# Attention scores of a two-block kernel on one core: every pair of heads' scores over all 128 rows of the array, with the residual h parked in DRAM to make room

## The chip, the core and the metric

The kernel runs on one core of one Trainium2 chip. Its program is written engine by engine: TensorE (PE) multiplies, VectorE (DVE) and ScalarE (ACT) work on the results, SyncE (SP) and GpSimd (POOL) issue the transfers, and semaphores tie them together. The metric is the device time of the core in microseconds, as the median of several executions; lower is better.

## What is computed

Two blocks run one after the other on 512 tokens of width 1024. The change lies in the first block, in its attention. Cut to that part:

```python
h = x
h = h + 0.5 * swiglu(rms_norm(h, ffn1_norm), ffn1_w1, ffn1_w3, ffn1_w2)
proj = rms_norm(h, mix_norm) @ w_in            # q, k, v of 12 heads of 64, pool input, gates
q, k = apply_partial_rope(q), apply_partial_rope(k)
for g, (window, dilation) in enumerate(((128, 1), (512, 4), (2048, 16))):   # 4 heads each
    s = q_g @ k_g.T * 64 ** -0.5               # banded and causal, key stride = dilation
    o_g, lse_g = softmax(s) @ v_g, log-sum-exp of s
o = sum_g softmax_g(lse_g) * o_g
h = h + (gate0 * (o @ w_branch_attn) + gate1 * (pool(proj) @ w_branch_pool)) @ w_out
h = h + 0.5 * swiglu(rms_norm(h, ffn2_norm), ffn2_w1, ffn2_w3, ffn2_w2)
```

All is float32 outside, and each product is made from two parts of each operand: a high part in a rounded float32 format (fp32r), and a low part that holds the rest. A product of split operands is three matmuls: high by high, high by low, low by high.

## The kernel before

**Stages.** The first feed-forward layer ends with h complete (tile h, 128 partitions x 8 x 512, 2 MB). Then comes the mixing stage. Its q and k columns are projected for three head groups g, once for the first pair of heads (a = 0, `qk(False)`) and once for the second pair (a = 1, `qk(True)`). Between them stand pool rows, values, and the attention of pair 0 (`attend(0)`); after the second come values and `attend(1)`. Then the gates and branches follow, in products of seven parts (`seven`), and a loop that adds the result into h.

**q and k.** For each g and each o (0 is q, 1 is k) PE projects 128 columns, both heads of the pair below each other, 64 rows each. ACT and DVE split the result (`rope_split`, `rope_low`) for two rotation matmuls (`rotate`), DVE multiplies by the cosine, and `rope_done` finishes the step: DVE multiplies and adds, ACT makes the high part, DVE the low part. In group 0 the high part is written by two ACT instructions of 64 rows into q_both[j] and k_both[j], one tile for each head j, and the low part by two DVE instructions into q_low and k_low. In groups 1 and 2 one ACT and one DVE instruction over 128 rows do it, into qk_hi and qk_lo. `prep` splits the next weight slab (ACT w_hi, DVE w_lo), and PE may not start on a slab before that. All of this is written out by hand, and each engine runs its own list strictly in order.

**Copies on POOL.** `other_halves(a)` fills the other 64 rows of q_both[j] with the low part of q, and those of k_both[j] with k's high part once more, so that one matmul over 128 rows gives (high + low of q) by (high of k). Four transfers of 128 KB from SBUF to SBUF do it, after group 0 of each pair.

**Scores.** `scores(a, k)` serves one unit, one head and one residue of the tokens by 4; there are 8 units for each pair, 16 in all. It makes 2 mask matmuls in bf16 (L2641, L2642), then for group 0 one over 128 rows (L2643) and one over 64 rows with k_low (L2644), and for groups 1 and 2 three each over 64 rows (L2419 to L2421, reached through `passes`): 10 matmuls. Units 0 and 1 stand between value matmuls, units 2 to 7 inside `attend`, which goes round once per unit: scores of unit k + 3, transposes of unit k + 1 (L2658), probabilities by values of unit k (L2683). ACT's list of a round is a quarter of a weight slab in the first four rounds (`prep_part`), two copies (`stage`), `normalizer` and `exps`; DVE has as much beside it.

**Queues.** SP issues the weight slabs in order, each when its place in the ring of two is free. POOL issues the adding transfers of the seven-part products (L571), the copies above, and copies into mix_b. Nothing reads or writes h between the end of the first feed-forward layer (with the scaling into x_hi and x_lo) and the loop that adds the mixing stage's result.

## Time and profile before

| | us |
|---|---|
| median of 3 runs | 1864.92 (1864.58 to 1866.64) |
| profiled execution | 1866.13, of which the span of its instructions 1864.1 |
| PE busy | 1850.0 (99%) |
| DVE busy | 1324.1 (71%) |
| ACT busy | 890.8 (48%) |
| POOL busy | 61.7 (3%) |
| DMA | 212.55 MB, mean 114 GB/s |
| granted TensorE clock | 0.998 |

Every row of the trace gives a start in microseconds from the beginning of the span, a duration, the engine, the line, the operation and its tiles; in square brackets stands how long the engine was idle before it and what ended that. Matmuls overlap one another, so the time that one takes on PE is read from the distance of the starts, not from its duration; the same holds for short DVE and ACT instructions, which overlap by about 0.1 us unless something holds them. The chain of waits is the chain of work that ended last: it goes through whichever engine was late at each moment.

### The profile page before, as it was taken

The numbers are of one execution on the slowest core, as the hardware profiler recorded it, in microseconds if no ns is written. First come the engines' busy times: TensorE is split into PE (matmuls) and PEld (weight loads), VectorE is DVE, ScalarE is ACT, GpSimd is POOL, SyncE is SP. The second block draws the span as 40 slices with busy tenths as digits, with TensorE's granted clock in tenths as the row PEclk, the third lists the DMA queues.
The fourth block names the chain that finished last, engine by engine and source line by source line (L and its number), as shares of the span: only waits on it lengthen the run. The fifth ranks groups of instructions, "written<-read, shape, count | busy, mean of one in ns | idle before, by whom it ended". The sixth has DMA issues, their size and how long they took to land.

```text
span 1864.1 us, 27146 instructions
## 1 busy us (share of the span) xinstructions
PE 1850.0 (99%) x10799; PEld 1627.6 (87%) x10799; DVE 1324.1 (71%) x1786; ACT 890.8 (48%) x1182; POOL 61.7 (3%) x80
## 2 busy tenths in 40 slices
PE   9999999999999999999999999999999999999997
PEld 7998998888889988989998888888888888888886
DVE  8875887887678889856888745463646776666666
ACT  6652664436365536634653342433336644444445
POOL 0000000010000000000000000000000000000000
PEclk9999999999999999999999999999999999999999
DMA  6744763341216426654753222122221222212213
GB/s 214 184 124 125 196 171 101 132 125 69 74 55 176 141 98 163 169 161 123 193 151 112 102 81 101 68 90 72 105 84 56 91 84 75 90 69 89 90 68 91
DMA packets 49633, 212.55 MB, mean 114 GB/s; under 512 B 5648, under 2 KB 8240, under 8 KB 38144
## 3 DMA queue, kind: packets, MB, share of 16 engines
q1 hardware_dynamic: 38816, 178.80, 28.1%
q0 software_dynamic: 10288, 31.84, 9.0%
q8 instruction: 68, 1.11, 0.2%
q10 hardware_dynamic: 432, 0.56, 0.1%
q14 instruction: 29, 0.24, 0.0%
HBM read 203.32 MB, written 3.67 MB: 111 GB/s over the span
## 4 chain that ended last, share of the span: by engine, by line
PE 94%; DVE 3%; ACT 1%; issue 1%; DMA 0%; DVEq 0%; ACTq 0%
PE acc L2419 20%; PE acc L2420 20%; PE acc L2421 20%; PE acc L2425 7%; PE acc L2426 7%; PE acc L2427 7%; PE att L2420 2%; PE att L2421 2%; PE att L2419 2%; PE att L2425 1%; PE att L2427 1%; PE att L2426 1%; PE acc L2683 1%; PE acc L2658 1%; DVE w_lo L1350 0%
## 5 line engine op out<-in xcount | busy, mean ns | idle before, releaser
L1350 DVE TENSOR_TENSOR w_lo<-raw,w_hi 128x2048 fp32r<-128x2048 f32 (+1 forms) x120 | 271.4, 2262 | 69.8 <-ACT w_hi L642 68.9
L642 ACT ACTIVATE w_hi<-raw 128x2048 fp32r<-128x2048 f32 (+1 forms) x120 | 226.5, 1888 | 120.4 <-PE acc L2421 105.6
L2419 PE MATMUL acc<-x_hi,w_hi 128*128 128x512 f32 x712 | 280.3, 394 | 0.3 <-DVE tmp L1578 0.3
L2421 PE MATMUL acc<-x_hi,w_lo 128*128 128x512 f32 x712 | 277.4, 390 | 0.0
L2420 PE MATMUL acc<-x_lo,w_hi 128*128 128x512 f32 x712 | 277.3, 389 | 0.0
L2419 PEld LDWEIGHTS acc<-x_hi,w_hi 128*128 128x128 f32 x712 | 133.7, 188 | 30.9 <-issue 2.7
L2420 PEld LDWEIGHTS acc<-x_lo,w_hi 128*128 128x128 f32 x712 | 133.7, 188 | 28.4 <-issue 1.2
L2421 PEld LDWEIGHTS acc<-x_hi,w_lo 128*128 128x128 f32 x712 | 133.6, 188 | 28.0
L2425 PE MATMUL acc<-xt_hi,w_hi 128*128 128x256 f32 x516 | 144.6, 280 | 0.0
L2427 PE MATMUL acc<-xt_hi,w_lo 128*128 128x256 f32 x516 | 144.3, 280 | 0.0
L2426 PE MATMUL acc<-xt_lo,w_hi 128*128 128x256 f32 x516 | 144.3, 280 | 0.0
L2420 PE MATMUL acc<-g_lo,w_hi 128*128 128x512 f32 x352 | 137.0, 389 | 0.0
L2419 PE MATMUL acc<-g_hi,w_hi 128*128 128x512 f32 x352 | 137.0, 389 | 0.0
L2421 PE MATMUL acc<-g_hi,w_lo 128*128 128x512 f32 x352 | 136.9, 389 | 0.0
L741 ACT ACTIVATE tmp<-acc 128x256 f32<-128x256 f32 x172 | 65.4, 380 | 78.9 <-PE acc L2427 71.4
L2425 PEld LDWEIGHTS acc<-xt_hi,w_hi 128*128 128x128 f32 x516 | 98.1, 190 | 0.0
L2426 PEld LDWEIGHTS acc<-xt_lo,w_hi 128*128 128x128 f32 x516 | 96.9, 188 | 0.0
L2427 PEld LDWEIGHTS acc<-xt_hi,w_lo 128*128 128x128 f32 x516 | 96.9, 188 | 0.0
L2425 PE MATMUL acc<-x_hi,wc_hi 128*128 128x256 f32 x344 | 95.1, 276 | 0.0
L2427 PE MATMUL acc<-x_hi,wc_lo 128*128 128x256 f32 x344 | 95.0, 276 | 0.0
L2426 PE MATMUL acc<-x_lo,wc_hi 128*128 128x256 f32 x344 | 95.0, 276 | 0.0
L2419 PEld LDWEIGHTS acc<-g_hi,w_hi 128*128 128x128 f32 x352 | 66.1, 188 | 13.7
(477 smaller groups left out, 4665.4 us busy)
## 6 DMA issues: line engine op xcount, KB each, us to landing
raw<-in_ret_head SPq DMA_DIRECT2D x24, 1024.0 KB, 4.8
raw<-in_ffn_down SPq DMA_DIRECT2D x32, 704.0 KB, 4.1
raw_c<-in_ffn_seven SPq DMA_DIRECT2D x37, 512.0 KB, 5.3
raw<-in_ffn_seven SPq DMA_DIRECT2D x33, 512.0 KB, 4.7
raw<-in_ffn_seven POOLq DMA_DIRECT2D x33, 512.0 KB, 7.5
raw<-in_ffn_seven SPq DMA_DIRECT2D x37, 256.0 KB, 4.5
raw<-in_ret_out SPq DMA_DIRECT2D x8, 1024.0 KB, 4.7
raw<-in_sb_v SPq DMA_DIRECT2D x8, 1024.0 KB, 4.7
```

The costliest lines, as they stand in the source:

```text
L642: nc.scalar.activation(w_hi[:, slot, at:at + cols], raw[:, slot, 0:cols], ACT.Copy).then_inc(w_hi_ready, 1)
L741: nc.scalar.activation(dst, src, ACT.Copy).then_inc(snap_ready, 1)
L1350: tt(w_lo[:, slot, at:at + cols], raw[:, slot, 0:cols], w_hi[:, slot, at:at + cols].bitcast(F32), ALU.subtract).then_inc(w_ready, 1)
L2419: mm(dst, still[0], move[0], start=first, stop=False)
L2420: mm(dst, still[0], move[1], start=False, stop=False)
L2421: return mm(dst, still[1], move[0], start=False, stop=last)
L2425: mm(dst, still[0], move[0], start=first, stop=False, skip_group_check=True)
L2426: mm(dst, still[0], move[1], start=False, stop=False, skip_group_check=True)
L2427: return mm(dst, still[1], move[0], start=False, stop=last, skip_group_check=True)
L2658: last = nc.tensor.transpose(dst[i // TB][:, P * (i % TB):P * (i % TB) + P], tmp[:, at:at + P], ident[:])
L2683: last = mm(dst, va[:, k_blk, value_slot(g, head)].rearrange("p s d -> p (s d)"), turned_probs[:, k % 2, i].rearrange("p s q -> p (s q)"), ...
```

## The change

All three groups are treated as group 0 was, and k's low part gets a second half of zeros, so that every scores product is two matmuls over 128 rows: (q high, q low) by (k high, k high), and (q high, q low) by (k low, zeros). That is 8 matmuls a unit in place of 10. q_both and k_both grow to three groups each. k_rest (the low part of k with zeros) and two of the three q_low tiles lie where h lies. So h is written to DRAM once it is complete (h_parked, 2 MB, by SP) and read back by POOL in four transfers of 512 KB between the adding transfers of the first four seven-part products. POOL also clears two halves of k_rest.

```diff
+        with ExitStack() as under:
+            k_rest = [sb(f"k_rest{j}", [P, N_GROUPS, TOK], F32R, under) for j in range(2)]
+            q_low = [sb(f"q_low{g}", [P, TOK], F32R, under) for g in range(N_GROUPS - 1)]
         h = sb("h", [P, DC, TOK])
+        h_parked = nc.dram_tensor("h_parked", (P, DC, TOK), F32, kind="Internal").ap()
...
         with ExitStack() as under:
-            k_low = sb("k_low", [P, TOK], F32R, under)
+            q_low.append(sb("q_low_last", [P, TOK], F32R, under))
...
             for g in range(N_GROUPS):
                 fetch(dram["mix_qk"][0, g])
+            sp.wait_ge(h_ready, DC)
+            sp.dma_start(h_parked, h[:]).then_inc(park_landed, 16)
...
+            pool.wait_ge(park_landed, 16)
+            pool.wait_ge(seg_done, FFN_SEGS[0] + 1)
+            for j, rows in enumerate(head_rows[::-1]):
+                nc.gpsimd.memset(k_rest[j][rows, :, :].bitcast(F32), 0.0).then_inc(rest_clear, 1)
...
                 own, other = head_rows, head_rows[::-1]
-                pool.wait_ge(both_ready, 2 * a + 1)
-                for j in range(2):
-                    pool.dma_start(q_both[j][other[j], :], q_low[own[j], :]).then_inc(both_landed, 16)
-                pool.wait_ge(both_ready, 2 * a + 2)
-                for j in range(2):
-                    pool.dma_start(k_both[j][other[j], :], k_both[j][own[j], :]).then_inc(both_landed, 16)
+                for g in range(N_GROUPS):
+                    done = 2 * (N_GROUPS * a + g)
+                    pool.wait_ge(both_ready, done + 1)
+                    for j in range(2):
+                        pool.dma_start(q_both[j][other[j], g, :], q_low[g][own[j], :]).then_inc(both_landed, 16)
+                    pool.wait_ge(both_ready, done + 2)
+                    for j in range(2):
+                        pool.dma_start(k_both[j][other[j], g, :], k_both[j][own[j], g, :]).then_inc(both_landed, 16)
...
                     add_pair(dram["mix_seven"][2 * j + k - MIX_PLAIN], slab)
                     v.next()
+                    if j < 3:
+                        pool.wait_ge(prob_ready, 2 * UNITS)
+                        rows = slice(2 * (2 * (j - 1) + k), 2 * (2 * (j - 1) + k) + 2)
+                        pool.dma_start(h[:, rows, :], h_parked[:, rows, :]).then_inc(h_back, 16)
...
-                if g:
-                    ins = nc.scalar.activation(qk_hi[:, o, g - 1, :], t(o), ACT.Copy, scale=QK_SCALE[o])
-                else:
-                    for j, rows in enumerate(head_rows):
-                        ins = nc.scalar.activation((k_both if o else q_both)[j][rows, :], t(o)[rows, :], ACT.Copy, scale=QK_SCALE[o])
+                for j, rows in enumerate(head_rows):
+                    ins = nc.scalar.activation((k_both if o else q_both)[j][rows, g, :], t(o)[rows, :], ACT.Copy, scale=QK_SCALE[o])
...
-                if g:
-                    stt(qk_lo[:, o, g - 1, :], t(o), QK_SCALE[o], qk_hi[:, o, g - 1, :].bitcast(F32), ALU.mult, ALU.subtract).then_inc(op_ready, 1)
-                else:
-                    for j, rows in enumerate(head_rows):
-                        stt((k_low if o else q_low)[rows, :], t(o)[rows, :], QK_SCALE[o], (k_both if o else q_both)[j][rows, :].bitcast(F32),
-                            ALU.mult, ALU.subtract).then_inc(both_ready if j else op_ready, 1)
-                    dve.wait_ge(both_ready, both.next())
+                if both.k == 0:
+                    dve.wait_ge(park_landed, 16)
+                for j, rows in enumerate(head_rows):
+                    dst, high = (k_rest[j][rows, g, :], k_both[j][rows, g, :]) if o else (q_low[g][rows, :], q_both[j][rows, g, :])
+                    stt(dst, t(o)[rows, :], QK_SCALE[o], high.bitcast(F32),
+                        ALU.mult, ALU.subtract).then_inc(both_ready if j else op_ready, 1)
+                dve.wait_ge(both_ready, both.next())
...
             rope_done(N_GROUPS - 1, 1, 0)
-            dve.wait_ge(both_landed, 4 * 16)
...
             sq.next()
+            dve.wait_ge(h_back, 4 * 16)
...
-                mm(wide, both[:, plain[r]], keys[:], start=False, stop=False)
-                mm(wide, both[rows, plain[r]], k_low[rows, :], start=False, stop=True)
-                for g in range(N_GROUPS - 1):
-                    last = passes(narrow[:, P * g:P * (g + 1)], (q[0][:, g, :], q[1][:, g, :]),
-                                  (qk_hi[rows, 1, g, plain[r]], qk_lo[rows, 1, g, plain[r]]), False, g == N_GROUPS - 2)
+                q, high, rest = q_both[head], k_both[head], k_rest[head]
+                mm(wide, q[:, 0, plain[r]], high[:, 0, :], start=False, stop=False)
+                mm(wide, q[:, 0, plain[r]], rest[:, 0, :], start=False, stop=True)
+                for g in range(1, N_GROUPS):
+                    dst = narrow[:, P * (g - 1):P * g]
+                    mm(dst, q[:, g, plain[r]], high[:, g, plain[r]], start=False, stop=False)
+                    last = mm(dst, q[:, g, plain[r]], rest[:, g, plain[r]], start=False, stop=g == N_GROUPS - 1)
...
                 pe.wait_ge(op_ready, op.at())
-                pe.wait_ge(both_landed, 4 * 16 * (a + 1))
+                pe.wait_ge(rest_clear, 2)
+                pe.wait_ge(both_landed, 4 * N_GROUPS * 16 * (a + 1))
                 scores(a, 0)
```

What it does to DVE's list at group 1 of q (a = 0), from the w_lo of the slab before to the next step; tmp holds the rotated q, L1374 is the low part of the next projection. Before:

```order
L1350 TENSOR_TENSOR w_lo<-raw,w_hi 128x2048 [waits w_hi_ready]
L1698 TENSOR_TENSOR tmp<-att,rope_a 128x512 [waits att_full]
L1701 TENSOR_TENSOR tmp<-tmp 128x512 [waits acc_free,att_free]
L1704 SCALAR_TENSOR_TENSOR qk_lo<-tmp,qk_hi 128x512 [waits hi_ready]
L1374 TENSOR_TENSOR stage<-acc,stage 128x512 [waits hi_ready,op_ready]
```

and after:

```order
L1362 TENSOR_TENSOR w_lo<-raw,w_hi 128x2048 [waits w_hi_ready]
L1710 TENSOR_TENSOR tmp<-att,rope_a 128x512 [waits att_full]
L1713 TENSOR_TENSOR tmp<-tmp 128x512 [waits acc_free,att_free]
L1719 SCALAR_TENSOR_TENSOR q_low<-tmp,q_both 64x512 [waits hi_ready]
L1719 SCALAR_TENSOR_TENSOR q_low<-tmp,q_both 64x512
L1386 TENSOR_TENSOR stage<-acc,stage 128x512 [waits hi_ready,op_ready,both_ready]
```

One instruction has become two of half the rows, and the next one waits for the second of them too; it is so at q and k of groups 1 and 2, four times for each pair.

PE's list at the first unit of a pair (`first_score`), masks first. Before:

```order
L2641 MATMUL att<-band,ident_b 128x512 [waits att_free,both_landed,op_ready]
L2642 MATMUL att<-classes,ident_b 128x256
L2643 MATMUL att<-k_both,q_both 128x512
L2644 MATMUL att<-k_low,q_both 128x512
L2419 MATMUL att<-qk_hi 128x128
L2420 MATMUL att<-qk_lo,qk_hi 128x128
L2421 MATMUL att<-qk_hi,qk_lo 128x128
L2419 MATMUL att<-qk_hi 128x128
L2420 MATMUL att<-qk_lo,qk_hi 128x128
L2421 MATMUL att<-qk_hi,qk_lo 128x128
```

and after:

```order
L2651 MATMUL att<-band,ident_b 128x512 [waits both_landed,att_free,rest_clear,op_ready]
L2652 MATMUL att<-classes,ident_b 128x256
L2654 MATMUL att<-k_both,q_both 128x512
L2655 MATMUL att<-k_rest,q_both 128x512
L2658 MATMUL att<-k_both,q_both 128x128
L2659 MATMUL att<-k_rest,q_both 128x128
L2658 MATMUL att<-k_both,q_both 128x128
L2659 MATMUL att<-k_rest,q_both 128x128
```

The two groups' three products have become two each, and the unit now waits for the copies of all three groups (the sizes are those of the outputs; the rows of the array don't show in them).

## Rows read from the trace of the kernel before

**Rows 1.** The page, busy time, share and instructions of each engine.

```profile
PE 1850.0 (99%) x10799; PEld 1627.6 (87%) x10799; DVE 1324.1 (71%) x1786; ACT 890.8 (48%) x1182; POOL 61.7 (3%) x80
```

**Rows 2.** Timeline of PE: one round of attend(0), then the transposes; start, duration.

```profile
445.57 0.39 PE L2641 MATMUL att<-band,ident_b 128*128 128x512 bf16 x1
445.80 0.27 PE L2642 MATMUL att<-classes,ident_b 128*128 128x256 bf16 x1
...
446.23 0.50 PE L2644 MATMUL att<-k_low,q_both 64*128 64x512 f32 x1
446.57 0.22 PE L2419 MATMUL att<-qk_hi 64*128 64x128 f32 x1
...
447.08 0.27 PE L2421 MATMUL att<-qk_hi,qk_lo 64*128 64x128 f32 x1
447.28 0.88 PE L2658 MATMUL acc<-ident,tmp 128*128 128x128 f32 x6
```

**Rows 3.** Timeline of DVE from the first rope_done to the value slab.

```profile
373.94 1.41 DVE L1707 SCALAR_TENSOR_TENSOR k_low<-tmp,k_both 64x512 fp32r<-64x512 f32 x2 [1.34 <-ACT k_both L875]
375.38 0.69 DVE L1374 TENSOR_TENSOR stage<-acc,stage 128x512 fp32r<-128x512 f32 x1
...
380.89 0.69 DVE L1704 SCALAR_TENSOR_TENSOR qk_lo<-tmp,qk_hi 128x512 fp32r<-128x512 f32 x1 [0.70 <-ACT qk_hi L872]
381.62 0.69 DVE L1374 TENSOR_TENSOR stage<-acc,stage 128x512 fp32r<-128x512 f32 x1
...
390.77 2.29 DVE L1350 TENSOR_TENSOR w_lo<-raw,w_hi 128x2048 fp32r<-128x2048 f32 x1 [1.11 <-ACT w_hi L642]
...
405.02 2.28 DVE L1350 TENSOR_TENSOR w_lo<-raw,w_hi 128x2048 fp32r<-128x2048 f32 x1
```

**Rows 4.** Timeline of PE: the first matmul on the value slab.

```profile
407.36 0.39 PE L2419 MATMUL acc<-w_hi,x_hi 128*128 128x256 f32 x1
```

**Rows 5.** Timeline of ACT: before the second pool slab, and between scores and values.

```profile
388.30 0.63 ACT L872 ACTIVATE qk_hi<-tmp 128x512 fp32r<-128x512 f32 x1 [2.92 <-DVE tmp L1701]
...
428.09 0.84 ACT L901 ACTIVATE va<-acc,r_tok 128x256 fp32r<-128x256 f32 x2 [0.81 <-PE acc L2421]
```

**Rows 6.** Timeline of ACT in attend(0): first and fourth quarter slab, then two stages.

```profile
441.47 0.62 ACT L652 ACTIVATE w_hi<-raw 128x512 fp32r<-128x512 f32 x1
...
450.43 0.64 ACT L652 ACTIVATE w_hi<-raw 128x512 fp32r<-128x512 f32 x1
...
454.25 0.60 ACT L931 ACTIVATE stage<-acc 128x512 fp32r<-128x512 f32 x1 [0.56 <-PE acc L2658]
...
457.11 0.60 ACT L931 ACTIVATE stage<-acc 128x512 fp32r<-128x512 f32 x1 [0.28 <-PE acc L2658]
```

**Rows 7.** Chain of waits through qk(True): start, duration, engine, tile, line.

```profile
471.66 0.47 issue
...
502.49 0.70 DVE qk_lo L1704
503.24 0.39 PE att L2641
```

**Rows 8.** Timeline of POOL, and the transfers of tile k_both: the copies.

```profile
375.64 1.03 POOL L596 DMA_DIRECT2D k_both<-k_both  x2 [4.21 <-DVE k_low L1707]
...
DMA to landing us min/median/max: 2.2/2.3/2.5
```

**Rows 9.** The last update of h; landing of 512 KB copies (mix_b); a POOL clear.

```profile
348.65 0.69 DVE L1633 TENSOR_TENSOR h<-h,tmp 128x512 f32<-128x512 f32 x1
...
DMA to landing us min/median/max: 3.4/6.8/13.7
...
1030.88 3.53 POOL L618 MEMSET y_ret<- 128x4096 f32 x1 [57.31 <-PE acc L2421]
```

**Rows 10.** Timelines of DVE and ACT at the second seven-part product.

```profile
581.42 1.22 DVE L1457 TENSOR_TENSOR w_lo<-raw,w_hi 128x1024 fp32r<-128x1024 f32 x1
...
586.10 0.36 ACT L741 ACTIVATE tmp<-acc 128x256 f32<-128x256 f32 x1
```

More of the change, by code:

```diff
@@ L127, in block_kernel @@
         x_lo = sb("x_lo", [P, DC, TOK], F32R)
-        with ExitStack() as under:
-            sb("tmp_first", [P, 4 * TOK], F32, under)
-            q_low = sb("q_low", [P, TOK], F32R, under)
         tmp = sb("tmp", [P, 6 * TOK])
         with ExitStack() as under:
-            k_low = sb("k_low", [P, TOK], F32R, under)
+            q_low.append(sb("q_low_last", [P, TOK], F32R, under))
         ssq = sb("ssq", [P, TOK])
@@ L252, in block_kernel @@
             with ExitStack() as inner:
-                q_both = [sb(f"q_both{j}", [P, TOK], F32R, inner) for j in range(2)]
-                k_both = [sb(f"k_both{j}", [P, TOK], F32R, inner) for j in range(2)]
-                qk_hi = sb("qk_hi", [P, 2, N_GROUPS - 1, TOK], F32R, inner)
-                qk_lo = sb("qk_lo", [P, 2, N_GROUPS - 1, TOK], F32R, inner)
+                q_both = [sb(f"q_both{j}", [P, N_GROUPS, TOK], F32R, inner) for j in range(2)]
+                k_both = [sb(f"k_both{j}", [P, N_GROUPS, TOK], F32R, inner) for j in range(2)]
                 va = sb("va", [P, TB, N_GROUPS * GROUP_HEADS, 2, HEAD], F32R, inner)
@@ L408, in block_kernel @@
         both_landed = sem("both_landed")
+        park_landed = sem("park_landed")
+        rest_clear = sem("rest_clear")
+        h_back = sem("h_back")
         mix_copied = sem("mix_copied")
@@ L2631, in scores @@
             def scores(a, k):
-                r, rows = k // 2, slice(HEAD * (k % 2), HEAD * (k % 2) + HEAD)
+                r, head = divmod(k, 2)
                 if k >= 2:
@@ L2638, in scores @@
                 b.next(2)
-                q = qk_hi[rows, 0, :, plain[r]], qk_lo[rows, 0, :, plain[r]]
-                both, keys = q_both[k % 2], k_both[k % 2]
                 mm(wide, ident_b[:], by_rows(band[:, DIL - 1 - r:2 * DIL - 1 - r, :]), start=True, stop=False)
                 mm(narrow[:, 0:2 * P], ident_b[:], by_rows(classes[:]), start=True, stop=False)
-                mm(wide, both[:, plain[r]], keys[:], start=False, stop=False)
-                mm(wide, both[rows, plain[r]], k_low[rows, :], start=False, stop=True)
-                for g in range(N_GROUPS - 1):
-                    last = passes(narrow[:, P * g:P * (g + 1)], (q[0][:, g, :], q[1][:, g, :]),
-                                  (qk_hi[rows, 1, g, plain[r]], qk_lo[rows, 1, g, plain[r]]), False, g == N_GROUPS - 2)
+                q, high, rest = q_both[head], k_both[head], k_rest[head]
[5 more added lines that the diff above has]
+                    last = mm(dst, q[:, g, plain[r]], rest[:, g, plain[r]], start=False, stop=g == N_GROUPS - 1)
                 last.then_inc(att_full, 2)
```

## The prediction

> **What bounds the kernel now.** I read the busy shares first, then the chain of waits over the mixing stage, then the timelines of PE, DVE and ACT at the places where the chain leaves PE. PE is busy 99% of the span and DVE 71% [rows 1], so nearly everywhere PE's own list sets the time. The average hides three places inside the mixing stage. In qk(False) PE doesn't visibly wait, but DVE has no slack to give: it runs its list through with no pause but its waits for ACT, its w_lo of the value slab ends at 405.02 + 2.28 = 407.30, and PE's first matmul on that slab starts at 407.36 [rows 3, 4]. In qk(True) the chain itself lies on DVE and ACT, from the end of the first projection at 471.66 to the last low part, 502.49 + 0.70 = 503.19; the first unit of pair 1 starts at 503.24 [rows 7]. In the first four rounds of attend ACT is full: from its first quarter slab at 441.47 to its fourth at 450.43 are three rounds of 2.99 us without a pause [rows 6].
>
> **What a unit of scores costs, and will cost.** Before, 1.71 us: 445.57 to 447.28 [rows 2]. Of this 0.23 and 0.43 are the two masks and the first group-0 product, which stay. The rest is 1.05 us: 0.34 for the 64-row product L2644, 0.51 from the first to the sixth narrow one (0.10 each), 0.20 from the sixth to the transposes. After: a 128-row product of 512 columns, for which I take the 0.23 of the mask of the same width, and four narrow ones at 0.11, together 0.67. Saving 0.38, call it 0.4. The bounds are 0.2 (only two narrow matmuls fewer, and the long steps round the 64-row products stay) and 0.55 (the 0.43 before them shrinks as well, and so does the first step of what follows). I stay near the middle, because the two long steps, 0.34 and 0.20, are just those where 64-row and 128-row matmuls meet, and after the change none meet. Sixteen units give 6.4 us if PE were the bound at all of them; it isn't.
>
> The Trainium skill, "TensorE: Matmul & The Clock Gate", section "Back-to-back issue gap", gives about 81 ns for a sustained matmul of 128 columns; the trace has 0.10 [rows 2], and by the page's figure a unit would save 0.1 us more, at the units that count about 0.3 us in all.
>
> **What the split into 64-row halves costs.** The pair at k of group 0 takes DVE from 373.94 to 375.38, 1.44 us, the single one of group 1 from 380.89 to 381.62, 0.73: 0.71 more. DVE waits 1.34 us for ACT's pair and 0.70 for the single copy: 0.64 more [rows 3]. So each `rope_done` of groups 1 and 2 costs DVE 1.35 us. There are four for each pair, eight in all.
>
> The Trainium skill, "VectorE: DVE Perf Modes", section "Two Vector instructions with no wait between them", says that an instruction whose output starts in another quarter of the partitions than the last is held until the earlier ones are done. The measured pair bears this out (1.44, two full durations of 0.69 and more). Without it two halves would follow one another as overlapping instructions do and the step would cost about 0.1 us less each; it speaks against the change.
>
> *Pair 0.* Three of the four steps cost 1.35. At the last but one, ACT makes w_hi of the second pool slab next, and DVE waits for that: 1.11 us of pause before 390.77 [rows 3]. ACT's own delay of 0.64 passes on (its copy at 388.30 becomes two [rows 5]), but DVE's 0.71 falls into the pause. Sum 3 x 1.35 + 0.65 = 4.7. The slack at 407.36 is 0.06, so PE stands still about 4.7 us, part of it already at the second pool slab. Then PE wins 0.8 on units 0 and 1, but the next link is ACT: its va at 428.09 had waited 0.81 for PE [rows 5], and ACT itself comes 4.7 later. 4.7 - 0.8 = **+3.9** either way.
>
> *attend(0).* Up to 441 the chain runs over ACT and DVE, and for three rounds more ACT is full, so faster scores give nothing there except what ACT's first pauses behind it show: 0.56 and 0.28 [rows 6]. **-0.85**; bounds 0 and 4 x 0.4 = 1.6 (PE bound in all four rounds that still have a scores call).
>
> *Pair 1.* Here DVE's chain is the path, and the four steps lie on it: **+5.4**. The rotation of group 2's q and of its k each start later, and PE pauses there instead of later. The last low part ends at 503.19 + 5.4 = 508.6. Before, PE started 0.05 behind it. Now k's last copies stand between: POOL starts 0.29 after the pair's end (373.94 + 1.41 to 375.64), two issues of 0.52, the second lands 2.3 after its start [rows 8]: 0.29 + 0.52 + 2.3 - 0.05 = **+3.05**. Queued behind PE's wait are unit 0, the third value block and all of attend(1), while DVE uses the time for its mix_b sums. Bounds 2.0 (if landing were counted with the first issue) and 5 (the copies of 512 KB on the same queue took 3.4 to 13.7 [rows 9], though nothing else of POOL's is under way here). Then units 0 and 1 of pair 1, on PE's path: **-0.8**. attend(1) as attend(0): **-0.85**.
>
> **h.** h is complete at 349.3 [rows 9], SP has nothing to wait for, and DVE's first low pair needs the place of h only at about 368.5, the step before 373.94 [rows 3]: 19 us for 2 MB. Four copies of 512 KB at the quickest 3.4 us make 13.6, and the new transfer has no other beside it at first. Nothing lost; at the median of 6.8 us each it would be 27, and DVE 8 us late. POOL's clear covers 1536 columns twice: from 3.53 us for 4096 [rows 9], 1.3 us each, while POOL waits for q anyway; lower bound 0, upper bound 2.6 before its first copy, which has 40 us until it is used. The way back adds 2 MB between the adding transfers. The second product's w_lo is ready at 582.6, and PE begins that product at about 584.7 (its first part, 12 matmuls of 256 columns or 1.4 us, is copied at 586.10) [rows 10]: 2 us of cover against transfers of the same size as those which it crosses. I take 0, upper bound 2. It also displaces the wait for both_landed on DVE, which the trace doesn't show as a pause: 0. Behind the mixing stage nothing changes, and PE is the bound, so what has been lost is kept.
>
> **Sum.** 3.9 - 0.85 + 5.4 + 3.05 - 0.8 - 0.85 = +9.85 us. The profiled execution took 1866.13, which is 1.2 above the median; its sum is 1876.0, and against the median 1864.92 + 9.85 = **1874.8**.
>
> **Rivals.**
> *Halves on the path, less the relief (1871.5).* As above, but the scores save 0.55 a unit and attend passes on nearly all of it: 1.6 + 0.6 for each attend in place of 0.85, and 0.6 more at units 0 and 1 of pair 1. For it: the long steps round 64 rows. Against it: ACT's three full rounds.
> *Transfers late (1879).* The forecast plus 2 to 6 us: copies of the last group that land at 4 us, a parking that ends behind 368.5, or the way back showing at a seven-part product. For it: the spread of 3.4 to 13.7 us. Against it: the small copies spread by 0.3 us only.
> *Not slower (1858.5).* DVE idles 29% of the span and POOL 97%. If the halves and copies ran in that idle time, only the 16 x 0.4 us would be left. It would take more than 4.7 us between w_lo and its use at 407, and more than 8 at 503. The rows show 0.06 and 0.05, so this decides against it; it is left only if DVE's list has play that a single trace hides, as where it waits for ACT.
>
> **How the numbers follow.** Forecast 0.62 (1872.5 to 1877.5), less cost 0.12 (0.02 of it below 1868.7), transfers late 0.17, not slower 0.09 (0.05 of it faster than 1861.2, 0.04 between that and 1868.7). 0.2% or 3.7 us is about what a measurement of this kernel can tell from no change. The range from 1870.5 to 1880.5 takes in the first three but for their tails. Slower 0.89, same 0.06, faster 0.05.
>
> **What would show it.** PE standing about 4.7 us before the value slab, w_lo being what ends it; the chain through qk(True) longer by 5.4; PE waiting some 3 us more for a copy into k_both before the first unit of pair 1; a unit of scores at 1.3 us; rounds of attend at 3.0. If the first unit of pair 1 starts less than 6 us later than by the shift that it inherits, or the rounds fall to 2.75, I am too high. If DVE waits for the parking, too low.

## The result, and the profile after

| | before | after |
|---|---|---|
| median, us | 1865.29 (1864.58 to 1866.64, 4 runs) | 1881.61 (1881.01 to 1882.52, 4 runs) |
| ratio, with its 95% interval | | 1.0087 (1.0070 to 1.0105) |
| span of the profiled execution | 1864.1 | 1879.4 |
| granted TensorE clock, mean | 0.998 | 0.993 |
| DMA, MB | 212.55 | 218.85 |

The change makes the kernel 16.3 us slower. The sign was forecast, the size was not: I had said +9.85, and 1881.6 lies above the range. The page after has nearly the same shares; POOL has 22 instructions more, and PE fewer busy microseconds in a longer span.

The page of after, busy time of each engine, for [rows 1]:

```profile
PE 1848.6 (98%) x10761; PEld 1629.8 (87%) x10767; DVE 1330.8 (71%) x1794; ACT 895.4 (48%) x1190; POOL 74.9 (4%) x102
```

The waits of PE in after (engine, tile, line, what ended them, us in total, times, longest). Of before the same view has 0.8 us in two pieces for the first of these, and neither of the other two:

```profile
PE att L2596 <- DVE stage L1386: 5.1, 3, 3.3
PE acc L2431 <- DVE w_lo L1362: 4.4, 1, 4.4
PE att L2652 <- DMA k_both<-k_both: 4.0, 1, 4.0
```

These are the standstills that the prediction names, at the places it names. The 4.0 reach to the second mask of the first unit, because the record of its first mask is missing; PE stood some 3.6 of them. ACT's copy of o_hi, which closes each pair of heads, shows where the time is lost. It starts at 466.14 and 541.84 before. After:

```profile
471.27 0.60 ACT L937 ACTIVATE o_hi<-att 128x512 fp32r<-128x512 f32 x1 [1.12 <-PE att L2639]
...
557.20 0.60 ACT L937 ACTIVATE o_hi<-att 128x512 fp32r<-128x512 f32 x1 [3.49 <-PE att L2639]
```

That is +5.13 for pair 0 and +15.36 for both, and the spans differ by 15.3. So all of it arises up to the end of attend(1), and nothing comes or goes behind it.

Now the timeline of PE in after at the value slab of pair 0, for [rows 4]; the first line is the last matmul on the slab before, and from 412.12 on each has 256 columns:

```profile
407.37 0.39 PE L2433 MATMUL acc<-x_hi,w_lo 128*128 128x512 f32 x1
412.12 0.58 PE L2431 MATMUL acc<-w_hi,x_hi 128*128 128x256 f32 x1 [4.37 <-DVE w_lo L1362]
...
412.93 0.41 PE L2431 MATMUL acc<-w_hi,x_hi 128*128 128x256 f32 x1
413.14 0.41 PE L2432 MATMUL acc<-w_lo,x_hi 128*128 128x256 f32 x1
...
425.23 0.28 PE L2432 MATMUL acc<-w_lo,x_hi 128*128 128x256 f32 x1
425.35 0.28 PE L2433 MATMUL acc<-w_hi,x_lo 128*128 128x256 f32 x1
```

The first starts 4.76 later than before (407.36), w_lo being what ends the wait: the 4.7 of the forecast. But behind it the matmuls start 0.21 apart, and only later 0.11. The view by stretches of after says why (stretch, its length, busy time of PE, PEld, DVE, ACT and POOL with counts, PEclk, DMA share, GB/s):

```profile
408.00:412.00 4.00, 0.00 (x0) 0.00 (x0) 3.86 (x7) 2.10 (x2) 3.09 (x3) 0.79 0.35 54
412.00:414.00 2.00, 1.88 (x9) 1.88 (x10) 1.89 (x4) 0.83 (x1) 0.80 (x1) 0.50 1.19 171
414.00:416.00 2.00, 2.00 (x11) 2.00 (x11) 1.90 (x4) 0.00 (x0) 0.00 (x0) 0.50 1.14 149
416.00:418.00 2.00, 2.00 (x15) 2.00 (x15) 1.61 (x4) 0.25 (x1) 0.00 (x0) 0.71 1.15 238
418.00:420.00 2.00, 2.00 (x20) 2.00 (x19) 1.08 (x1) 0.86 (x1) 0.00 (x0) 1.00 1.25 201
```

While PE stood still its granted clock fell to 0.50, that is 1.2 in place of 2.4 GHz, and it stayed there for some 5 us of work: 9 to 11 matmuls in 2 us where the last line counts 20 at 1.00. In before the clock is 1.00 in every stretch from 406 to 420. The Trainium skill, "TensorE: Matmul & The Clock Gate", section "What's actually happening", describes just this: a gate in front of the array that halves its clock when PE has had nothing to do, and opens again under work. The trace agrees, and my prediction did not use it. The same view of after in pair 1:

```profile
510.00:512.00 2.00, 2.00 (x12) 2.00 (x11) 1.23 (x2) 0.69 (x2) 0.00 (x0) 0.50 0.40 79
...
516.00:518.00 2.00, 0.01 (x1) 0.14 (x3) 2.00 (x4) 0.00 (x0) 0.00 (x0) 0.53 0.35 72
518.00:520.00 2.00, 2.00 (x8) 1.80 (x8) 0.44 (x2) 0.00 (x0) 0.00 (x0) 0.50 0.00 0
520.00:522.00 2.00, 2.00 (x11) 2.00 (x11) 0.96 (x1) 0.89 (x2) 0.00 (x0) 0.50 0.00 0
522.00:524.00 2.00, 2.00 (x16) 2.00 (x14) 0.00 (x0) 0.10 (x2) 0.00 (x0) 0.76 0.03 8
```

The clock falls twice more: behind 3.29 us of waiting for DVE (up to 508.9), where DVE's chain is the path and a slow PE does little harm, and behind the wait for k's copies, where the first unit of scores and a value block run at half the rate with nothing to hide them.

A unit of scores in after, in the timeline of PE, for [rows 2]; the record of its first mask is missing, and the block before it ends with a matmul that starts at 425.35:

```profile
425.69 0.27 PE L2652 MATMUL att<-classes,ident_b 128*128 128x256 bf16 x1
425.72 0.48 PE L2654 MATMUL att<-k_both,q_both 128*128 128x512 f32 x1
426.04 0.39 PE L2655 MATMUL att<-k_rest,q_both 128*128 128x512 f32 x1
426.27 0.22 PE L2658 MATMUL att<-k_both,q_both 128*128 128x128 f32 x1
...
426.55 0.27 PE L2659 MATMUL att<-k_rest,q_both 128*128 128x128 f32 x1
426.66 0.33 PE L2431 MATMUL acc<-w_hi,x_hi 128*128 128x256 f32 x1
```

From 425.46 (0.11 behind that matmul) to 426.66 are 1.20 us, against 1.71 before. The Trainium skill, "TensorEngine Tiling (Array Packing)", section "Key Properties", states that a change of the tiling mode drains the array. The rows agree: the step of 0.34 at the 64-row product is 0.23 now, and the 0.20 behind the last narrow one is 0.11. No run changes the mode alone, with the number of matmuls kept.

The account of the mixing stage, forecast against trace:

| step | forecast | trace | how read |
|---|---|---|---|
| PE stands before the value slab | +4.7 | +4.76 | 407.36 to 412.12 |
| low clock behind it | none | +1.93 | to unit 0: 13.34 after, 11.41 before |
| units 0 and 1, pair 0 | -0.8 | -1.12 | va at 433.66 instead of 428.09 is +5.57 in all |
| attend(0) | -0.85 | -0.44 | +5.57 to +5.13 |
| qk(True), DVE's chain | +5.4 | +5.69 | last low part ends at 514.01, before 503.19 |
| k's last copies | +3.05 | +3.54 | first unit at about 517.6, 3.6 behind it |
| units 0 and 1, attend(1) | -1.65 | -1.56 | taken as in pair 0 |
| low clock behind the copies | none | +2.56 | what is left: 15.36 less the rows above, see below |
| sum | +9.85 | +15.36 | |

The last two rows are not read each by itself. A direct reading supports them: from the first unit of pair 1 to the second are 6.55 us in after (517.57 to 524.12) and 4.05 in e6_early_copy (517.25 to 521.30), the same work at a clock of 1.00, so the low clock cost 2.5 there. The +1.93 is a difference from before; e3_warm, with the clock at 1.00, does the same four value blocks in 11.0 us and not 11.4, and against that the low clock cost 2.3. Why its matmuls stand 0.113 us apart and those of before 0.118, both at 1.00, no run shows.

Of the 5.5 us between forecast and trace, 4.5 are the two rows that the forecast lacks.

### The profile page after: what moved, and what is told of

Its sections match the earlier page's. It is cut to its first block, busy times and chain, and to the rows that moved or that the text cites. A ratio compares the mean times of both kernels' runs of the same rounds, so it can differ in the third digit from the quotient of the medians.

```text
span 1879.4 us, 27122 instructions
## 1 busy us (share of the span) xinstructions
PE 1848.6 (98%) x10761; PEld 1629.8 (87%) x10767; DVE 1330.8 (71%) x1794; ACT 895.4 (48%) x1190; POOL 74.9 (4%) x102
## 2 busy tenths in 40 slices
DMA packets 51633, 218.85 MB, mean 116 GB/s; under 512 B 5984, under 2 KB 8576, under 8 KB 40016
## 4 chain that ended last, share of the span: by engine, by line
PE 72%; DVE 6%; ACT 2%; issue 1%; DMA 0%; DVEq 0%; POOL 0%
PE acc L2431 16%; PE acc L2433 16%; PE acc L2432 16%; PE acc L2438 4%; PE acc L2437 4%; PE acc L2439 4%; PE att L2432 2%; PE att L2433 2%; PE att L2431 2%; DVE w_lo L1362 1%; PE att L2437 1%; PE att L2439 1%; PE att L2438 1%; DVE neg_max L1753 1%; DVE tmp L1713 0%
## 5 line engine op out<-in xcount | busy, mean ns | idle before, releaser
L2431 PE MATMUL acc<-w_hi,x_hi 128*128 128x512 f32 (+1 forms) x224 | 79.6, 355 | 4.4 <-DVE w_lo L1362 4.4
```

The lines of the kernel that those rows point to most:

```text
L2431: mm(dst, still[0], move[0], start=first, stop=False)
```

## Experiments

Each kernel ran beside the kernel before on the same chip. Differences are of medians; the interval is that of the ratio to before. The last column compares medians that were not taken side by side: the kernel before itself lay between 1865.1 and 1865.9 in these rounds, so differences there are good to somewhat under 1 us. The edits are shown in part.

| kernel | median, us | ratio to before | against before | against after |
|---|---|---|---|---|
| e1_park | 1866.56 | 1.0003 (0.9993 to 1.0012) | +0.7 | |
| e2_halves | 1877.84 | 1.0064 (1.0047 to 1.0080) | +12.0 | -3.8 |
| e3_warm | 1877.75 | 1.0063 (1.0046 to 1.0080) | +11.9 | -3.9 |
| e5_relief | 1863.18 | 0.9984 (0.9974 to 0.9993) | -2.7 | |
| e4_stagger | 1873.89 | 1.0043 (1.0026 to 1.0060) | +8.4 | -7.7 |
| e6_early_copy | 1877.66 | 1.0063 (1.0046 to 1.0080) | +12.1 | -4.0 |
| e7_all_three | 1871.41 | 1.0029 (1.0016 to 1.0042) | +5.9 | -10.2 |
| e8_before_step | 1864.79 | 0.9995 (0.9986 to 1.0005) | -0.7 | |
| e9_pool_half | 1875.15 | 1.0049 (1.0032 to 1.0066) | +9.3 | -6.5 |
| e10_stagger_early | 1872.54 | 1.0034 (1.0021 to 1.0046) | +6.7 | -9.1 |
| e11_stagger_early_warm | 1871.53 | 1.0033 (1.0021 to 1.0044) | +5.7 | -10.1 |
| e12_no_standing | 1869.94 | 1.0027 (1.0015 to 1.0038) | +4.8 | -11.7 |

### The parts, each by itself on the kernel before

The parking alone:

```
+            sp.wait_ge(h_ready, DC)
+            sp.dma_start(h_parked, h[:]).then_inc(park_landed, 16)
...
+                    if j < 3:
+                        pool.wait_ge(prob_ready, 2 * UNITS)
+                        rows = slice(2 * (2 * (j - 1) + k), 2 * (2 * (j - 1) + k) + 2)
+                        pool.dma_start(h[:, rows, :], h_parked[:, rows, :]).then_inc(h_back, 16)
```

> The kernel before with only the parking of h: the 2 MB copy to DRAM behind the third mix_qk slab on SP, the four copies back between POOL's adding transfers, DVE's two waits for them. Nothing of the scores changes. My theory (the transfers are hidden, all of the loss is made of DVE's halves, the wait for k's copies and TensorE's lower clock behind both): within 0.5 us of before. Rival (the 4 MB more of traffic cost something in slabs that land later, or in the way back): 2 to 6 us slower, with a new DMA or h_back wait on DVE or PE. The changed kernel itself shows no such wait, so I expect the first.

Measured +0.7 with an interval of -1.3 to +2.2 us, and in the profile no wait of PE or DVE for a transfer of h. The 4 MB cost nothing that can be told.

The split alone (ACT likewise):

```
-                    stt(qk_lo[:, o, g - 1, :], t(o), ...).then_inc(op_ready, 1)
+                    for j, rows in enumerate(head_rows):
+                        stt(qk_lo[rows, o, g - 1, :], t(o)[rows, :], ...).then_inc(both_ready if j else op_ready, 1)
```

> The kernel before with only the split: groups 1 and 2 get their high part (ACT) and low part (DVE) in two halves of 64 rows each, with DVE's wait for the second; scores, copies and h as before. Theory: PE stands still about 4.8 us before the first value slab, the granted clock is 0.50 behind it and the four value blocks take 1.9 us more; in pair 1 the chain through DVE is 5.5 us longer, and there is no wait for copies. Sum 4.8 + 1.9 + 5.5 = +12.2 us, about 1877. Rival A (the clock has nothing to do with the standstill, but with the copies or the 128-row scores): granted clock 1.00 behind it, +10.3, about 1875. Rival B (halves hide in idle time): within 1 us of before.

Measured +12.0, where the theory had +12.2. The interval, +8.8 to +14.9, rules out rival B but would hold rival A's +10.3; what speaks against A is the granted clock, which falls behind the wait although the scores still run over 64 rows and no copy is added. The timeline of PE and the stretches around it in e2_halves:

```profile
412.37 0.58 PE L2422 MATMUL acc<-w_hi,x_hi 128*128 128x256 f32 x1 [4.34 <-DVE w_lo L1351]
```

```profile
412.00:414.00 2.00, 1.63 (x7) 1.63 (x8) 1.89 (x4) 1.08 (x1) 0.00 (x0) 0.50 0.28 71
414.00:416.00 2.00, 2.00 (x14) 2.00 (x13) 1.93 (x3) 0.00 (x0) 0.00 (x0) 0.67 0.17 65
416.00:418.00 2.00, 2.00 (x20) 2.00 (x19) 1.81 (x5) 0.02 (x1) 0.00 (x0) 1.00 0.00 0
```

Here it lasts some 3 us, in the profile of after 5: the price of the same wait varies. The pieces of this profile are 5.0 of standing, 1.1 of low clock (ACT's o_hi of pair 0 starts 6.16 later than before) and 5.5 in pair 1 (o_hi there 11.66 later).

The relief on PE alone:

```
...
-                mm(wide, both[rows, plain[r]], k_low[rows, :], start=False, stop=True)
+                mm(wide, both[:, plain[r]], k_low[:, :], start=False, stop=True)
...
-                    last = passes(narrow[:, P * g:P * (g + 1)], (q[0][:, g, :], q[1][:, g, :]),
-                                  (qk_hi[rows, 1, g, plain[r]], qk_lo[rows, 1, g, plain[r]]), False, g == N_GROUPS - 2)
+                    dst = narrow[:, P * g:P * (g + 1)]
+                    mm(dst, qk_hi[:, 0, g, plain[r]], qk_hi[:, 1, g, plain[r]], start=False, stop=False)
+                    last = mm(dst, qk_hi[:, 0, g, plain[r]], qk_lo[:, 1, g, plain[r]], start=False, stop=g == N_GROUPS - 2)
```

> The kernel before with only the relief on PE: a unit of scores issues the changed kernel's matmuls (two of 512 columns and four of 128, all over 128 rows) on the tiles that the kernel before has. This leaves out part of the computation: groups 1 and 2 sum over both heads of a pair and lack one low product, and group 0's low product takes rows of both heads. Nothing else changes. Theory: a unit takes 1.2 to 1.3 us in place of 1.71; units 0 and 1 of pair 0 give 0.8 (then ACT is the bound), attend(0) 0.45, units 0 and 1 of pair 1 give 1.1, attend(1) 0.45: -2.8 us, about 1862.5. My forecast's terms sum to -3.3. Rival (PE is the bound at all sixteen units): 16 x 0.45 = -7.2, about 1858.

Measured -2.7, the theory's -2.8. So this is what the change has to give: 0.45 to 0.5 us a unit, of which 16 units let a third through. The three parts add up to +10.0. The change is +16.3; the 6.3 between are put down to the copies, 3.5 of waiting and 2.6 of low clock by the account above. That is a difference of runs, with the spread of each in it; no run adds the copies alone.

### The clock, by itself

PE is given matmuls whose result nobody reads while it would stand still:

```
+            def keep_busy(n):
+                pe.wait_ge(att_free, b.at(1))
+                for i in range(n):
+                    mm(att[:, b.k % BANKS, :], rot_r[:], x_hi[:, i % DC, :], start=True, stop=True)
...
+                if behind:
+                    keep_busy(14)
                 pe.wait_ge(op_ready, op.at(behind))
...
+            keep_busy(17)
             values(x, plain)
...
+                if a:
+                    keep_busy(26)
                 pe.wait_ge(op_ready, op.at())
```

> The changed kernel, with matmuls whose result nobody reads put where PE stands still: 17 of 512 columns before the first value slab of pair 0, 14 before the last rotation of pair 1, 26 before its first scores. No one's work moves otherwise. Theory (the granted clock fell to 0.50 because PE stood still, and this costs 1.9 us behind the value slab and 2.6 us behind the wait for k's copies): clock near 1.00 at both places and 4 to 5 us faster than the changed kernel, about 1877. Rival (the lower clock there has another cause, or costs nothing since others set the time): 1881 to 1882, or slower where the added matmuls run past the end of the wait.

Measured -3.9 against after, and the executions don't overlap (1877.6 to 1878.6 against 1881.0 to 1882.5). The timeline of PE in e3_warm, and its stretches there and in pair 1:

```profile
408.24 4.12 PE L2632 MATMUL att<-x_hi,rot_r 128*128 128x512 f32 x17
412.71 0.39 PE L2431 MATMUL acc<-w_hi,x_hi 128*128 128x256 f32 x1 [0.34 <-DVE w_lo L1362]
```

```profile
412.00:414.00 2.00, 1.66 (x13) 1.29 (x12) 1.89 (x4) 1.43 (x1) 1.41 (x2) 1.00 1.21 182
...
518.00:520.00 2.00, 2.00 (x19) 2.00 (x19) 0.96 (x1) 0.50 (x1) 0.00 (x0) 1.00 0.00 0
```

The value slab still comes when DVE has made it, at 412.7, but what follows runs at 1.00 at once. This settles that the clock falls because PE stands still, and that the low clock costs about 4 us on top of the standstills. It is a lower bound: the 26 matmuls before the first scores of pair 1 run on until 517.0, while the second copy is issued at 513.81 and in after PE starts 2.4 behind that issue, so some 0.8 us of them are too many. The 57 added matmuls, whose result nobody reads, make the kernel faster.

### Where the halves cost: ACT and DVE one behind the other

```
-                    ins = nc.scalar.activation((k_both if o else q_both)[j][rows, g, :], ...)
-                ins.then_inc(hi_ready, 1)
+                    nc.scalar.activation((k_both if o else q_both)[j][rows, g, :], ...).then_inc(half_ready[j], 1)
...
-                dve.wait_ge(hi_ready, hi.next())
...
                 for j, rows in enumerate(head_rows):
+                    dve.wait_ge(half_ready[j], both.k + 1)
```

> The changed kernel, but DVE no longer waits for both of ACT's halves before its own: each half of ACT raises a semaphore of its own, and DVE starts the first low half while ACT makes the second high half. The halves stay as many and as long. Theory (the 1.35 us a step of my forecast is made of 0.64 of waiting and 0.71 of DVE work, and the path runs through both): each of the twelve steps gives 0.6 to 0.65 back, in pair 0 at least five of six, so PE stands still about 1.5 us in place of 4.8 and the clock stays at 1.00 behind it, 3.2 + 1.9; in pair 1 six steps, 3.7; the wait for k's copies and the low clock behind it stay. Sum -8.8 us against the changed kernel, about 1872.8. Rival (it is DVE's work alone that counts, waiting hides): under 1 us.

Measured -7.7 against after where -8.8 was expected. The timeline of DVE in e4_stagger, beside [rows 3]: the pair is as long as before, the wait ahead of it is 0.70 in place of 1.34.

```profile
373.12 1.41 DVE L1719 SCALAR_TENSOR_TENSOR k_rest<-tmp,k_both 64x512 fp32r<-64x512 f32 x2 [0.70 <-ACT k_both L888]
```

And PE's wait at the value slab is half as long (timeline of PE):

```profile
410.03 0.39 PE L2431 MATMUL acc<-w_hi,x_hi 128*128 128x256 f32 x1 [2.21 <-DVE w_lo L1362]
```

The miss of 1.1 is the clock again: I had expected none to be lost behind this shorter wait. It fell, and the four value blocks behind it take 12.6 us (410.03 to 422.66) against 11.4 in before:

```profile
410.00:412.00 2.00, 1.97 (x11) 1.97 (x12) 1.89 (x3) 0.73 (x1) 1.60 (x2) 0.61 1.22 186
412.00:414.00 2.00, 2.00 (x11) 2.00 (x11) 1.90 (x4) 0.00 (x0) 0.00 (x0) 0.53 1.17 158
```

### k's copies

```
-                    pool.wait_ge(both_ready, done + 2)
                     for j in range(2):
+                        pool.wait_ge(half_ready[j], done + 2)
...
+                pe.wait_ge(both_ready, 2 * N_GROUPS * (a + 1))
                 pe.wait_ge(both_landed, 4 * N_GROUPS * 16 * (a + 1))
```

> The changed kernel, but k's copies on POOL wait for ACT's high halves, which they copy, and no longer for DVE's low halves behind them; PE waits for those itself. Theory (the copies' latency lies on the path before the first unit of pair 1): both copies start earlier by DVE's two halves of 0.72, so PE's wait for k_both shrinks from 4.0 to 2.6 us: -1.4 us, about 1880; and if the shorter standstill keeps the clock at 1.00 behind it, another -2.6, about 1877.5. Rival (something else holds PE there): no change.

Measured -4.0, which is the larger of the two cases, but by other pieces. In the profile the second copy is issued 2.1 us sooner against DVE's last low part than in after, since the first no longer waits for ACT's second half either, and PE stands 1.4 us in place of some 3.6 (waits of PE; here the first mask is on record); behind that the clock is 1.00 (stretches):

```profile
PE att L2652 <- DMA k_both<-k_both: 1.4, 1, 1.4
```

```profile
516.00:518.00 2.00, 0.75 (x4) 0.61 (x5) 1.97 (x2) 0.74 (x2) 0.00 (x0) 1.00 0.28 56
```

The 2.1 and the 2.6 of the clock would be 4.7. In this profile PE reached the value slab of pair 0 0.9 later than in after, which I can't explain, and the clock stayed low for longer behind it (some 6 us), so that o_hi of pair 0 comes 1.4 later; pair 1 by itself is 4.2 shorter than in after.

### Together, and what they uncover

The move of the first two units:

```
-            values(x, plain, {(0, DC - 1): lambda: rotate_last(1), (1, DC - 1): lambda: first_score(1),
-                              (2, DC - 1): lambda: scores(1, 1)})
+            values(x, plain, {(0, DC - 1): lambda: rotate_last(1), (2, DC - 1): lambda: first_score(1),
+                              (3, DC - 1): lambda: scores(1, 1)})
```

> The changed kernel with the staggered halves, k's early copies, and in pair 1 the first two units of scores one value block later (behind the third and fourth block in place of the second and third), so that a block of 2.7 us lies under the copies' latency. Theory: -8.8 of the stagger, -1.4 of the early copy, -2.6 of the block under what remains of the wait, and -2.6 since the clock no longer falls: 1881.6 - 15.4 = 1866, level with the kernel before. Rival (the losses overlap, so that taking one away uncovers the next): 1869 to 1873. A further rival: the later first unit leaves ACT too little time before the first transposes of attend(1), 1 to 2 us given back.

Measured 1871.4, not 1866: both rivals came. The timeline of PE at the start of attend(1) in e7_all_three:

```profile
517.55 0.87 PE L2670 MATMUL acc<-ident,tmp 128*128 128x128 f32 x6 [0.89 <-ACT tmp L928]
521.32 0.84 PE L2670 MATMUL acc<-ident,tmp 128*128 128x128 f32 x6 [1.53 <-DVE va L1438]
```

The wait for the copies is gone (0.3 us are left), but with the first unit one block later ACT and DVE are late for the first transposes by 2.4 us. A third wait of 0.95 follows at 523.1, and behind these three the clock falls, though none of them is longer than 1.53:

```profile
522.00:524.00 2.00, 1.05 (x6) 0.92 (x5) 1.87 (x5) 1.93 (x5) 0.00 (x0) 0.69 0.00 0
```

In the 2 us after these it is 0.50. It fell behind the 2.22 us before the value slab too (0.53 and 0.61 in the two stretches from 410). The sum of 15.4 had put down nothing for either.

> The changed kernel with the staggered halves and k's early copies, units of scores where they were. Theory (the wait for k's copies, and the clock behind it, come on top of the halves): the same 4 us less than with the stagger alone as the early copies gave on the changed kernel: 1873.9 - 4 = 1870. Then moving the first units of pair 1 one block later has brought nothing or lost 1 us (1871.4), since the wait it removed came back in front of attend(1). Rival (the move was worth its 2 us): 1873.

Measured 1872.5 with executions from 1869.8 to 1873.4, between the two cases: the median says that the move of the units was worth 1.1 us, the spread says that this isn't shown. In the profile PE stood 2.2 us before the value slab as in e4_stagger, and this time kept its clock:

```profile
410.00:412.00 2.00, 1.61 (x13) 1.61 (x14) 1.89 (x4) 1.11 (x1) 1.55 (x2) 1.00 1.23 185
412.00:414.00 2.00, 2.00 (x19) 2.00 (x18) 1.93 (x3) 0.00 (x0) 0.00 (x0) 1.00 1.16 152
```

Up to there this kernel and e7_all_three are the same. So at this length of wait the fall comes in one execution and not in another. The four executions of e9_pool_half show what may hang on it: 1873.35 and 1874.61 us at a mean clock of 0.998, 1875.69 at 0.996 and 1876.95 at 0.995. Only the last has a trace; its waits before the value slab, the last rotation and the first scores are 4.6, 2.5 and some 3.4 us.

> The same, with matmuls whose result nobody reads in the two standstills that are left: 8 of 512 columns before the value slab of pair 0 (2.2 us of waiting there), 7 before the last rotation of pair 1 (2.0 us). Theory (the clock fell to 0.50 behind the 2.2 us, and that alone costs 1.5 to 2 us there): the clock stays at 1.00 and the time falls by 1.5 to 2 us against the same kernel without them, to about 1868. Rival (at 2 us the low clock costs nothing on the path): no difference.

Measured -1.0 against e10_stagger_early, with ranges that overlap: not shown either way. This run could hardly show it: in the profile of e10_stagger_early the clock was kept at that place without added matmuls, and the wait for the copies was left open (3.4 us, clock 0.50 behind it).

> The kernel with staggered halves, early copies and added matmuls at two places, with 14 more of 512 columns before the first scores of pair 1, where PE still stood 3.4 us and the granted clock was 0.50 behind it. Theory (the spread of 3 us between executions of the kernels with staggered halves, 1870.4 to 1873.2, comes from the clock, which falls behind such a wait in some executions for longer than in others): mean clock 0.998 as before, all executions within about 1 us, median 1869.5 to 1870. If the halves and copies cost nothing but what is left of DVE's chain, this is the floor of the change as it is, 4 us above the kernel before. Rival (the spread has another cause, or the low clock is no loss there): the median stays at 1871.5 and the spread at 3 us.

Measured 1869.9, mean clock 0.998 to 0.999 in all seven executions; six lie between 1869.5 and 1870.6. The seventh, 1871.9, had the full clock too, so the clock isn't the whole of the spread. 4.8 us above before remain. The median is 1.6 below that of e11_stagger_early_warm (0.9 with each taken against its own kernel before), and the ranges overlap in part (1869.5 to 1871.9 and 1870.4 to 1873.2). In the profile ACT's o_hi starts at 467.44 and 546.08, 1.3 and 4.2 later than before: pair 0 is nearly even, and in pair 1 what is left of DVE's chain and the copies' latency outweighs the relief; how the two share it no run shows.

### Half of the work on POOL

```
+                    nc.gpsimd.tensor_tensor(q_low[g][rows, :], t(0)[rows, :], q_both[1][rows, g, :].bitcast(F32), ALU.subtract)
...
+                    nc.gpsimd.tensor_tensor(k_rest[1][rows, g, :], t(1)[rows, :], k_both[1][rows, g, :].bitcast(F32), ALU.subtract)
```

> The changed kernel with the staggered halves and k's early copies, and with the second low half of each step (of q and of k) on POOL in place of DVE; q's scale of 1/8 moves from ACT's and DVE's halves into DVE's two steps before them, an exact power of two. DVE waits for POOL's half before it writes the buffer that POOL reads. Theory (what counts is DVE's time a step: one wait of 0.7 for ACT's first half and one low half of 0.7 are 1.4, as much as before in groups 1 and 2 and half of it in group 0): no wait for w_lo before the value slab, clock 1.00 there, and pair 1's chain 3 us shorter than before, with some 2 us of wait for k's copies left. About 1861 to 1865, if POOL needs no more than about 1 us for 64x512 elements (its clear took 1.4 us for 128x1536, a simpler operation). Rival (POOL needs 2 us or more, and DVE waits for it, six times in each pair): every further us costs about 10; 1870 or more.

Measured 1875.2, inside the rival's range though POOL needs less than its 2 us, so not for its reason alone. POOL's half takes 1.3 us (groups of instructions on POOL: shapes, count, busy us, mean ns, idle before), against 0.7 on DVE, and DVE waits for it and for ACT (timeline of DVE):

```profile
L615 POOL TENSOR_TENSOR k_rest<-tmp,k_both 64x512 fp32r<-64x512 f32 x6 | 7.9, 1324 | 0.1
```

```profile
386.59 0.69 DVE L1393 TENSOR_TENSOR stage<-acc,stage 128x512 fp32r<-128x512 f32 x1 [0.66 <-ACT stage L686]
388.27 0.69 DVE L1710 TENSOR_TENSOR tmp<-acc,rope_a 128x512 f32<-128x512 f32 x1 [0.99 <-POOL k_rest L615]
```

The 0.66 is there as well: with its own second half gone, DVE comes to the next step before ACT has finished its two copies and that step's high part. ACT's pair costs time on DVE's path even with DVE's second half gone. How the rest of the time divides is not shown.

### The staggered halves on the kernel before

> The kernel before with the staggered halves alone, in its group 0, where it has them already: two steps in each pair. Theory (in pair 1 the path runs through ACT's and DVE's steps, in pair 0 PE has no wait to lose): 2 x 0.6 = -1.2 us, about 1864.5, at the limit of what can be told from no change. Rival (all four count): -2.5, about 1863.

Measured -0.7, interval 0.9986 to 1.0005, which is -2.6 to +0.9 us: it holds the theory's -1.2, the rival's -2.5 and no change alike, and decides nothing. No kernel here is measurably faster than the one before but e5_relief, which leaves out part of the computation.

## Why the prediction was too low

**What bounds the kernel, and where it waits.** Right at all three places: PE stopped where [rows 4] had 0.06 us of slack and [rows 7] had 0.05, and DVE's w_lo, DVE's chain and the copy ended the waits. The rival "not slower" is refuted by e2_halves, the rival "transfers late" by e1_park for the parking and the way back, and by the trace of after for k's last copy, which landed in 2.2 us: its time, 1879, is near, but its mechanism isn't there. The rival "less the relief" had the size of a unit right (0.55, measured 0.51), but attend passed on less and not more.

**The split.** Right: +4.76 for 4.7, +5.69 for 5.4. The chain of waits shows the step at q of group 1 in qk(True), first before (start, duration, engine, tile, line), 1.4 us from ACT's copy to the end of DVE's low part:

```profile
490.71 0.64 ACT qk_hi L872
...
491.37 0.70 DVE qk_lo L1704
```

and then after, two copies of ACT and two low parts of DVE in a row, the 2.7 us that the steps of group 0 had in [rows 3]:

```profile
495.85 0.63 ACT q_both L887
...
496.49 0.64 ACT q_both L887
...
497.15 0.69 DVE q_low L1719
...
497.88 0.69 DVE q_low L1719
```

**The step that failed** is "PE stands still about 4.7 us" (pair 0) and "Before, PE started 0.05 behind it. Now k's last copies stand between" (pair 1). Both price a standstill at its own length, and go on with matmul durations read at a clock of 1.00. I named a page of the Trainium skill for the distance of matmuls and passed over what the same page says of the clock. The trace of before couldn't show it, since the longest wait of PE in its whole span is 1.5 us; but a standstill three times as long was then outside what the trace shows, and the work behind it should have had two bounds, its durations as read and twice these. What the runs showed in its place is a granted clock of 0.50 behind both standstills, worth 1.93 + 2.56 us; e3_warm gives 3.9 of it back.

**attend.** -0.85 each, measured -0.44. I had read that ACT is full in the first rounds. DVE is as well: its neg_max comes every 2.99 us with not one pause, as the timeline of DVE in after shows:

```profile
450.25 0.94 DVE L1753 TENSOR_REDUCE neg_max<-att 128x1 f32<-128x768 f32 x1
...
453.23 0.94 DVE L1753 TENSOR_REDUCE neg_max<-att 128x1 f32<-128x768 f32 x1
```

**A unit of scores** gave 0.51, inside the bounds, nearer the upper one, in place of the 0.4 in the sum: I had kept the 0.43 at the first group-0 product, which is 0.35 after.

**k's copies.** +3.05, measured 3.54: between the two issues on POOL lay 0.35 us of its own, which I had taken from a pair that shows none. The landing was 2.2, as in [rows 8].

**h.** Nothing, as forecast. The 2 MB landed 8.2 us behind their issue at 349.3, inside the 19 us.

## What to carry to other kernels

When PE comes to stand still for some microseconds in a stage where it is otherwise full, count the wait and then about half as much again for the work behind it at 1.2 GHz (1.9 us behind 4.4 and 2.5 behind 3.6 here); if the wait can't be avoided, fill it with matmuls on data at hand, and no more of them than the wait is long. Before giving PE shorter work, look at whether PE is the bound at each place where that work stands: sixteen units that each became 0.5 us shorter were worth 2.7 us, and the four steps a pair that paid for them lay on engines without slack. Where one engine makes halves for another, let it signal each of them: 7.7 of the 16.3 us came back by that alone (e4_stagger), the low clock that it spared included.

## What the runs showed of the hardware

- Behind a standstill of 4.3 to 4.4 us before the value slab the granted clock was 0.50 for some 3 us of work in one profile (e2_halves), 5 in another (after) and 6 in a third (e6_early_copy). Behind 2.2 us it fell in the profiles of e4_stagger and e7_all_three and stayed at 1.00 in that of e10_stagger_early. Behind 2.0 us before the last rotation it stayed at 1.00 in all three, and behind 1.4 us in e6_early_copy.
- The length of a single wait doesn't decide it: in e7_all_three the clock fell to 0.50 behind three waits of 0.89, 1.53 and 0.95 us (between 516.7 and 523.1, with transposes and a unit of scores in between).
- A unit of scores took 1.71 us with its products over 64 rows beside masks over 128, and 1.20 with all over 128. Two narrow matmuls fewer are 0.2 of the 0.5; what is left comes where the changes between the two were, and no run takes them apart.
- A subtraction over 64x512 elements takes 1.3 us on POOL and 0.7 on DVE. The Trainium skill, "GPSIMD Engine Reference", section "4.1 Engine selection", puts POOL at about half of DVE's rate for operations with two inputs; the rows agree.
